# Two attention stages of a two-block network: where the weight unit of the latent query, the key inputs of differential attention and the steps of its last head stand in the engines' queues

## The reference, cut to what matters

```python
q = (rmsnorm(c_q, g_q_lat) @ w_uq).reshape(b, s, 8, 128 + 64)
k_nope = (c_kv @ w_uk).reshape(b, s, 8, 128); v = (c_kv @ w_uv).reshape(b, s, 8, 128)
sc = (q_nope @ k_nope.T + rope(q_rope) @ k_rope.T) * (128 + 64) ** -0.5
p = softmax(where(mask, sc, -inf));  o = p @ v
y = (silu(gate) * o) @ w_out
```

```python
q = h @ w_q;  k, v = split(rms_norm(x, g_kv) @ w_kv)
probs = softmax(where(causal, q @ k.T * 64 ** -0.5 + bias, -inf))       # for m = 0, 1
attn = probs[:, 0] - lam * probs[:, 1];  o = rms_norm(attn @ v, subln_g) * (1 - lambda_init)
mix = o @ w_o
```

## Time and profile before

| | us |
|---|---|
| median of three runs | 2021.4 (2021.33 to 2022.42) |
| the profiled execution | 2021.45 |
| its span, first to last instruction | 2019.7 |
| TensorE busy (matmuls) | 1964.7, 97% of the span |
| VectorE, ScalarE, GpSimd busy | 1251.6, 834.2, 310.0 |
| latent attention's heads | from 530.9 to about 662 |
| differential attention's heads | from 1373.6 to about 1543 |

### The profile page before, as it was taken

The page is one execution under the profiler, slowest core; times in us unless marked ns, Lnnn a source line. Parts: engine busy times, 40 slices in busy tenths (PEclk is TensorE's granted clock), DMA queues, the critical chain, the costliest instruction groups (busy, mean ns, idle before and its releaser), DMA issues.

```text
span 2019.7 us, 27332 instructions
## 1 busy us (share of the span) xinstructions
PE 1964.7 (97%) x10578; PEld 1684.7 (83%) x10578; DVE 1251.6 (62%) x2227; ACT 834.2 (41%) x1391; POOL 310.0 (15%) x249
## 2 busy tenths in 40 slices
PE   8999999999899999999999999999999999999997
PEld 7898888887787987898888889887887988888896
DVE  6675666267565573467777623786663778775256
ACT  5233323244465432254444323555554444442343
POOL 1322332101232100010111110111112011110101
PEclk9999999999999999999999999999998999999998
DMA  4323222223111233323223322233111323233321
GB/s 167 95 79 98 84 81 92 84 84 96 63 35 50 86 98 109 118 74 105 78 100 104 126 94 77 81 105 107 44 47 59 105 79 99 97 102 116 101 70 60
DMA packets 54967, 179.02 MB, mean 89 GB/s; under 512 B 6295, under 2 KB 10903, under 8 KB 54840
## 3 DMA queue, kind: packets, MB, share of 16 engines
q1 hardware_dynamic: 54840, 177.29, 27.3%
HBM read 172.55 MB, written 4.72 MB: 88 GB/s over the span
## 4 chain that ended last, share of the span: by engine, by line
PE 65%; DVE 6%; ACT 3%; issue 2%; POOL 1%; DVEq 0%; ACTq 0%; POOLq 0%
PE pb L827 62%; DVE WL L808 1%; ACT WH L797 1%; PE pb L927 1%; PE pb L2700 1%; PE pb L2229 1%; PE pb L911 0%; DVE X L1008 0%; DVE T L2974 0%; ACT T L1864 0%; DVE FD L999 0%; DVE FR L2935 0%; PE pb L1744 0%; PE pb L2745 0%; PE pb L915 0%
## 5 line engine op out<-in xcount | busy, mean ns | idle before, releaser
L827 PE MATMUL pb<-FR,WH 128*128 128x512 f32 (+1 forms) x5100 | 1450.9, 370 | 16.4 <-DVE FR L1583 6.6
L827 PEld LDWEIGHTS pb<-FR,WH 128*128 128x128 f32 x5100 | 917.8, 189 | 177.5 <-issue 14.5
L827 PE MATMUL pb<-FR,WL 128*128 128x512 f32 (+1 forms) x2550 | 937.9, 368 | 0.0
L808 DVE TENSOR_TENSOR WL<-stage,WH 128x1024 fp32r<-128x1024 f32 (+1 forms) x311 | 401.2, 1307 | 410.9 <-ACT WH L797 409.8
L827 PEld LDWEIGHTS pb<-FR,WL 128*128 128x128 f32 x2550 | 482.7, 189 | 80.4
L797 ACT ACTIVATE WH<-stage 128x1024 fp32r<-128x1024 f32 (+1 forms) x311 | 319.4, 1050 | 114.4 <-PE pb L827 101.3
L827 PE MATMUL pb<-WH,FR 128*128 128x256 f32 x832 | 156.4, 285 | 1.4 <-DVE WL L808 1.4
L827 PEld LDWEIGHTS pb<-WH,FR 128*128 128x128 f32 x832 | 132.1, 192 | 2.6 <-DVE WL L808 2.0
L827 PE MATMUL pb<-FR 128*128 128x256 f32 (+3 forms) x752 | 123.6, 315 | 7.5 <-POOL FR L2140 4.5
L827 PEld LDWEIGHTS pb<-FR 128*128 128x128 f32 x752 | 111.8, 194 | 21.9 <-POOL FR L2140 5.6
L1284 POOL TENSOR_TENSOR acc<-acc,T 128x512 f32<-128x512 f32 (+1 forms) x53 | 63.6, 1200 | 418.2 <-ACT T L1255 275.1
(11 more groups left out here) (229 smaller groups left out, 1661.0 us busy)
## 6 DMA issues: line engine op xcount, KB each, us to landing
stage<-in_ws SPq DMA_DIRECT2D x310, 512.0 KB, 3.6
X<-in_xT SPq DMA_DIRECT2D x8, 256.0 KB, 6.5
FD<-in_decay SPq DMA_DIRECT2D x8, 256.0 KB, 3.8
FD<-scr SPq DMA_DIRECT2D x1, 2048.0 KB, 8.2
out_dram<-X SPq DMA_DIRECT2D x16, 128.0 KB, 1.7
scr<-FD SPq DMA_DIRECT2D x10, 160.0 KB, 5.1
FD<-in_rope_b SPq DMA_DIRECT2D x2, 512.0 KB, 3.5
FD<-in_pT SPq DMA_DIRECT2D x4, 256.0 KB, 5.5
```

The lines of the kernel that those rows point to most:

```text
L808: dve.tensor_tensor(lo, src, hi.bitcast(F32), ALU.subtract).then_inc(*self.tick("w_lo", ("w_lo", u)))
L827: m = pe.matmul(out, l, r, start=first and i == 0, stop=last and i == n - 1)
```

## The change

In `lat`, the `hi_to` and `lo_to` of the query's block leave `query`. On ScalarE the call stands behind the exponential of scores(h,3), on VectorE behind turn(h,0) and turn(h,1). In head 7, where there is no next query, the call for the output projection's units moves likewise. In `dif`, all eight key inputs stand at the entry's end; in head 7 ScalarE makes one unit ahead of the exponentials of block 2 and one ahead of those of block 3, and VectorE takes scores(7,2) and finish(5) ahead of combine(7,0), and makes the last unit ahead of combine(7,2). Nothing is computed that was not computed before, and TensorE's, GpSimd's and SyncE's lists are as they were.

```diff
# act_lat
         def query(h):
             head("q", h, self.lat_qn)
-            self.hi_to(act, BLOCK["w_uq", 2, nope_q(h)])
...
         query(0)
+        self.hi_to(act, BLOCK["w_uq", 2, nope_q(0)])
         key(0)
...
             divide(h, 2)
             if after:
                 query(h + 1)
+            scores(h, 3)
+            if after:
+                self.hi_to(act, BLOCK["w_uq", 2, nope_q(h + 1)])
             else:
                 out("head 7, e")
-            scores(h, 3)
             if h:
                 values(h - 1)
             turn(h, 0)
# dve_lat
         def query(h):
             head("q", h, self.R, ("r", "lat", "cq"))
-            self.lo_to(dve, BLOCK["w_uq", 2, nope_q(h)])
...
         query(0)
+        self.lo_to(dve, BLOCK["w_uq", 2, nope_q(0)])
         key(0)
...
             if after:
                 query(h + 1)
-            else:
-                out("head 7, e")
             scores(h, 3)
             if h:
                 values(h - 1)
             invert(h, 3)
             turn(h, 0)
             turn(h, 1)
+            if after:
+                self.lo_to(dve, BLOCK["w_uq", 2, nope_q(h + 1)])
+            else:
+                out("head 7, e")
             if h and even:
                 value(h)
             turn(h, 2)
# act_dif
-        self.act_entry(act, "dif", BLOCK["w_q_2", KD - 1, 6], spare=lambda: [key_input(k) for k in range(4)],
+        self.act_entry(act, "dif", BLOCK["w_q_2", KD - 1, 6], spare=lambda: [key_input(k) for k in range(KD)],
...
         self.hi_to(act, BLOCK["w_q_2", KD - 1, 7])
-        for k in range(4, KD):
-            key_input(k)
         query(6)
...
             if h >= 2:
                 finish(h - 2)
+            if h == 7:
+                out(DIF_OUT["head 7, c"])
             scores(h, 2)
             if h < 7:
                 key(h + 1)
             else:
-                out(DIF_OUT["head 7, c"])
                 rounded(5)
+                out(DIF_OUT["turn"])
             scores(h, 3)
             if h:
                 values(h - 1)
...
-            else:
-                out(DIF_OUT["turn"])
# dve_dif
-        for k in range(4):
+        for k in range(KD):
             key_input(k)
...
         self.lo_to(dve, BLOCK["w_q_2", KD - 1, 7])
-        for k in range(4, KD):
-            key_input(k)
         query(6)
...
             scores(h, 1)
-            combine(h, 0)
-            if h >= 2:
+            if h < 7:
+                combine(h, 0)
+                if h >= 2:
+                    finish(h - 2)
+                scores(h, 2)
+                key(h + 1)
+                scores(h, 3)
+            else:
+                scores(h, 2)
                 finish(h - 2)
-            scores(h, 2)
-            if h < 7:
-                key(h + 1)
-            else:
+                combine(h, 0)
                 out(DIF_OUT["head 7, c"])
-            scores(h, 3)
+                scores(h, 3)
+                out(DIF_OUT["turn"])
...
             else:
-                out(DIF_OUT["turn"])
                 turn(h, 0)
                 turn(h, 1)
```

More of the change, by code:

```diff
@@ L2905, in act_dif @@
                 values(h - 1)
+            turn(h, 0)
+            turn(h, 1)
             if h < 7:
                 c = (h + 1) // 2
-                turn(h, 0)
-                turn(h, 1)
                 value(c, [(h + 1) % 2])
```

## The result

The changed kernel takes 2007.65 us (median of six runs, 2007.09 to 2010.81) beside 2021.37 for the kernel before on the same chip (2019.28 to 2023.83): ratio 0.9934, interval 0.9923 to 0.9944. It is faster by 0.66%, 13.7 us. Predicted were 2012.0 us and a range of 2007.0 to 2018.0. The profiled execution took 2008.05, its span is 2006.3.

What follows compares the result with a forecast made beforehand. TensorE, with matmuls in 97% of the span, was taken as the bound, so only its idle and clock could be won. Gains of 4.7 latent, 1.2 key inputs and 3.6 head 7 made 9.5: 2021.45 to 2012.0 us, range 2007.0 to 2018.0.

Steps and rivals of the forecast that it cites:

- The query's unit: Latent heads 0, 1, 3, 6: block 3's exponential starts 3.0 us earlier, division ends 2.0 earlier, TensorE's wait at turn(h,3) goes.
- The key inputs: Entry of differential attention: the unit's low part is ready before TensorE's first value pair wants it; 1.2 us go.
- Head 7's new waits: Differential attention, head 7: new TensorE waits of 1.4 (rounded head 5), 1.1 (square of head 6) and 0.5 us (VectorE's sums_of(6)).
- the chain in the latent heads: ScalarE's and VectorE's head-to-head chain gains 0.9, 1.2, 1.2 in heads 0, 1, 3, together 3.3 us, and TensorE with it.
- head 6's value pair: Latent head 6: value pair evacuated 1.3 us earlier, TensorE's 1.2 of idle goes, 1.4 against the distance of neighbours.
- The latent sum: Latent stage: 3.3 from the chain plus 1.4 in head 6 makes 4.7 us; bounds 2.0 and 5.9.
- the clock in head 7: Differential attention, head 7: 5.6 us at high clock, less 2.0 for one 4.7 us low stretch: 3.6; bounds 2.4 and 5.6.
- rival (B): Clock doesn't fall in differential attention's head 7 (2010.0 us), nor perhaps in latent head 6 (2006.6); chance 0.22.
- VectorE's order: Differential attention, head 7: VectorE reads block 2 ahead of combine(7,0) and finish(5), so TensorE starts scores(7,3) 2.0 us earlier.
- The sum: Whole kernel: 4.7 latent, 1.2 key inputs and 3.6 head 7 make 9.5 us, giving 2012.0; as summed, chance 0.57.
- (C): Waits move to GpSimd's at scores(h+1,0), and head 7's low clock and waits eat its 2.0: 2018.9 to 2021 us; chance 0.15.
- (D): Slower: units delay the division in latent heads and head 7 where the exponential comes less than 1.04 earlier; 2031.6 us; chance 0.06.

Runs made afterwards that it cites:

- the experiment with VectorE's half: Kernel before with only VectorE's latent low part moved, ScalarE's high part left in place: 2013.33 us beside 2023.30, ratio 0.9955.
- the half pair: Changed kernel with latent head 5's unit moved and ScalarE evacuating the value pair's first half ahead of the division: 2007.42 us, ratio 0.9924 to the kernel before.

## Why the prediction was right, and where not

**Right in its mechanisms.** *The query's unit:* the exponential of block 3 was to start at 554.5, which is 552.65 less the 1.85 us of lead already there; it started at 552.64. The division was to end 2.0 earlier and TensorE not to wait: both hold. That VectorE's place decides was right, the experiment with VectorE's half shows it. *The key inputs:* 1.2 predicted, 1.27 measured, twice. The bias table left 2.7 us later, counted from TensorE's position (1356.66 with a lead of 6.3, against 1360.23), and nothing waited for it; ScalarE's 3.70 us of idle became 1.24. *Head 7's new waits:* 1.4, 1.1 and 0.5 predicted, 1.17, 0.84 and under 0.3 in the rows; against the distance of neighbours the first two are 1.38 and 1.05.

**Mis-sized: the chain in the latent heads.** The step "the chain gains 0.9 in head 0, 1.2 in head 1, 1.2 in head 3" is 3.3; measured were 1.05, 2.17 and 2.36, less 0.78 and 0.75 for value pairs in heads 3 and 5: 4.05. The chain's own figure held: the maximum of scores(2,0) comes at 557.73 instead of 560.82, which is 1.24 beyond the lead of 1.85. The step that failed is "and TensorE with it". TensorE kept all of what its own wait lost in heads 1 and 3, and the chain presented its bill one head later, in a place that I had not named: for the value pair's bank, not in GpSimd's waits at scores(h+1,0).

**Mis-sized, and covered by luck: head 6's value pair.** Predicted were 1.4 us, all of the wait; 0.8 went, and 0.40 is left in the row. The step "the value pair is evacuated 1.3 earlier" holds for ScalarE's half: it starts at 627.72 instead of 634.55, 1.35 beyond the lead of 5.48. VectorE followed 0.87 behind ScalarE before and could have at 628.6, but in its new place the unit's low part stands ahead of the pair and holds it to 629.16, which is 0.8 beyond the lead. Head 6 as a whole still gave 1.45, close to the 1.4, because 0.65 came from elsewhere in it (shorter waits and the clock). The sign "no idle for the value pair of latent head 6" didn't come. The latent sum was 5.5 instead of 4.7: 0.75 more from the chain, 0.6 less from the pair, 0.65 from the rest of head 6.

**Mis-sized: the clock in head 7.** "I count one low stretch of 4.7 us, 2.0, and take 3.6." This profile had none and gave 5.8, a little above the upper bound of 5.6, which was rival (B)'s first half; the same kernel's second profile had 3.4 us and gave 4.6; with head 7 alone it was 6.8 us and 3.1, with latent head 5's unit moved, without and with the half pair, 3.4 us and 4.3 and 4.2. So 3.6 lies inside what this code does, below the average of the five, 4.4, and what I took for a price is a spread. The lower bound of 2.4 was wrong by its own row: 0.42 of 10.2 us is 4.3, and 5.6 less 4.3 is 1.3. The row's 0.42 of the length held: 1.2 us between the changed kernel's two profiles for 3.4 us (0.35), 1.5 for 3.4 where no wait hides any of it (0.45). The Trainium skill, "TensorE: Matmul & The Clock Gate", part 1, gives 0.5; the latent stretches come near it, those that lie over waits do not, and where the estimate by it was 7.1 us for head 7 at the high clock, 5.8 were measured.

**Right, but for one part a wrong reason.** VectorE's order was put down as the edit that starts TensorE 2.0 us earlier. It does, and 0.6 of it lasts. The units' new place, which I had costed as what keeps new waits short, is the part that carries head 7: alone it gave a ratio of 0.9970, VectorE's order alone 0.9990, and without VectorE's order the changed kernel is as fast as with it, within the intervals.

**The sum.** 9.5 were predicted; the change's own part of this pair of profiles is 12.6: 0.8 more in the latent heads, 0.1 at the key inputs, 2.2 in head 7. The remaining 0.8 of the spans' 13.4 are the start and the stage's entry, and another 0.4 the median's distance from the profiled execution. So the forecast's miss of about 4.3 us is 3.1 in the change, as this pair of profiles has it, and 1.2 outside it. Of rival (B) the first half came in one of the two profiles; the second didn't, latent head 6 has 6.8 and 3.4 us of low clock. Rivals (C) and (D) fell: GpSimd's waits didn't grow, and the exponential came more than 1.04 earlier. The three parts alone gave 8.1, 3.0 and 3.0 us by their ratios, 14.1, so they add up to the whole, 13.7, within their intervals, which are wide: 5.7 to 10.3, 1.2 to 4.7 and 1.0 to 4.9.

## What to carry to other kernels

Where a step is moved ahead of another in a queue, follow the chain until its slack is used up, and name what TensorE meets last there: in head 7 three orders of the same steps had 2.0 to 2.7 us of idle, in other places. In the latent heads what paid was to put a step that nobody waits for behind the one that is waited for, on the engine where it stood idle for its own input. Low stretches of TensorE's clock come and go between executions of one kernel, so a gain read from two profiles is good to 1.5 us for each stretch more or less: take such stretches out before comparing, and leave the rest to repeated runs.

## What the runs showed that I had not expected

The same waits do or don't bring the clock down: with 1.17 and 0.84 us of idle in head 7 it stayed at 2.4 GHz in one execution, and with 1.19 and 0.84 it fell to 1.2 GHz for 3.4 us in another. The 1.94 us waits of latent heads 1 and 3 had no low stretch in the profile of before and one of 3.4 us each in that of the kernel with head 7 alone.

A low stretch can pay part of its own price. In the kernel with the units alone the 12 matmuls of values(6) took 3.10 us instead of 2.10 and the waits behind them were zero; with the same order at the high clock, in the changed kernel with VectorE's order undone, they took 2.12 and were followed by waits of 0.59 and 0.20.

VectorE's low part of a unit took 1.22 us in head 7 of the changed kernel and, in its latent heads, 1.22 or 1.44 to 1.45. In head 1 the longer one (555.89) overlaps the end of a GpSimd step of 1.30 us (554.96 to 556.26). In the entry of differential attention, beside GpSimd's low parts of the queries, it took 1.91 and 2.33.
